# Seven products of half tiles in the last block of a gated-branch layer

## The reference

```python
h = rmsnorm(x, g_pre); proj = h @ w_in                 # 1024 x 10240
out_a = gmlp_spatial(a_u, layernorm(a_v)) * silu(a_z)
out_b = silu(layernorm(depthwise31(b_a * sigmoid(b_b)))) * silu(b_z)
out_c = multiscale_pool(c_x) * silu(c_z)
out_d = d_b * depthwise3(d_c * d_x) * silu(d_z)
merged = sum_i sigmoid(gate_i + b_i) * (out_i @ w_branch[i])   # 4 gates of width 1024
x + rmsnorm(merged @ w_out, g_post)                    # and the new states of the convolutions
```

## Time and profile before

| | |
|---|---|
| median of three runs | 2459.53 us |
| profiled execution, its own time | 2460.2 us |
| its span | 2458.1 us |
| PE busy (matmuls) | 2434.8 us, 99% |
| VectorE busy | 1258.1 us, 51% |
| ACT, POOL busy | 393.5 us, 329.2 us |
| mean rate of the DMAs | 215 GB/s |

### The profile page before, as it was taken

One profiled execution on the slowest core, in us unless ns is written; L12 is line 12 of the kernel. 1 busy time (PEld: TensorE's weight loads), 2 busy tenths in 40 slices (PEclk: granted clock), 3 DMA queues, 4 the chain that ended last, 5 costly groups with the idle time before them and its releaser, 6 DMA issues.

```text
span 2458.1 us, 34054 instructions
## 1 busy us (share of the span) xinstructions
PE 2434.8 (99%) x12772; PEld 2116.8 (86%) x12772; DVE 1258.1 (51%) x1923; ACT 393.5 (16%) x602; POOL 329.2 (13%) x173
## 2 busy tenths in 40 slices
PE   9999999999999999999999999999999999999998
PEld 7888887788888888888888888888899999999997
DVE  6776878752535455643344455654144545554323
ACT  5222222323011000111101000010201100000101
POOL 5435444444000000001000000000200000000000
PEclk9999999999999999999999999999999999999999
DMA  8868887787644555555654555555554344444457
GB/s 320 313 240 298 299 297 283 256 291 268 242 177 171 205 202 207 207 180 205 250 194 163 200 198 217 185 197 197 211 199 156 131 168 177 149 165 171 151 181 280
DMA packets 120382, 528.57 MB, mean 215 GB/s; under 512 B 11664, under 2 KB 14096, under 8 KB 74192
## 3 DMA queue, kind: packets, MB, share of 16 engines
q1 hardware_dynamic: 106032, 502.21, 57.1%
q10 hardware_dynamic: 14240, 24.89, 2.8%
HBM read 409.02 MB, written 118.03 MB: 214 GB/s over the span
## 4 chain that ended last, share of the span: by engine, by line
PE 96%; DVE 2%; issue 1%; DVEq 0%; POOL 0%; DMA 0%; ACT 0%; POOLq 0%; ACTq 0%
PE acc L1231 82%; PE acc L1474 6%; PE side L1369 4%; PE acc L1334 1%; PE side L1396 1%; PE side L1386 1%; PE side L1256 0%; DVE cb L791 0%; PE acc L1375 0%; PE side L1277 0%; DVE tmp L1026 0%; POOL w_pair L402 0%; DMA col<-in_cols 0%; DVE sq_y L1124 0%; DVE merged L1029 0%
## 5 line engine op out<-in xcount | busy, mean ns | idle before, releaser
L1231 PE MATMUL acc<-h_hi,w_pair 128*128 128x512 f32 (+1 forms) x5984 | 1553.3, 353 | 0.0
L1231 PEld LDWEIGHTS acc<-h_hi,w_pair 128*128 128x128 f32 x5984 | 1027.0, 188 | 142.3 <-issue 3.6
L1231 PE MATMUL acc<-h_lo,w_pair 128*128 128x512 f32 (+1 forms) x2992 | 951.4, 351 | 0.0
L1231 PEld LDWEIGHTS acc<-h_lo,w_pair 128*128 128x128 f32 x2992 | 529.3, 188 | 72.2 <-issue 3.6
L791 DVE SCALAR_TENSOR_TENSOR cb<-glu,col,cb 128x512 f32<-128x512 f32 x600 | 396.1, 725 | 23.2 <-issue 18.6
L1231 PE MATMUL acc<-out_hi,w_pair 128*128 128x512 f32 (+1 forms) x1280 | 346.5, 352 | 5.0 <-DVE tmp L1026 5.0
L402 POOL TENSOR_TENSOR w_pair<-w_raw,w_pair 128x512 fp32r<-128x512 f32 (+1 forms) x119 | 272.2, 2299 | 278.5 <-ACT w_pair L500 264.8
L1231 PEld LDWEIGHTS acc<-out_hi,w_pair 128*128 128x128 f32 x1280 | 221.3, 188 | 36.1 <-DVE tmp L1026 6.3
L1026 DVE TENSOR_TENSOR tmp<-acc,sig 128x512 f32<-128x512 f32 (+1 forms) x96 | 68.0, 708 | 342.2 <-PE acc L1231 340.3
L416 POOL TENSOR_TENSOR rstd<-msq,nhalf 128x5 f32<-128x5 f32 (+3 forms) x18 | 19.1, 1063 | 1648.0 <-DVE msq L725 797.7
L510 ACT ACTIVATE sig<-acc,col 128x512 f32<-128x512 f32 (+1 forms) x128 | 90.0, 703 | 896.3 <-PE acc L1231 894.3
(11 more groups left out here) (173 smaller groups left out, 1458.9 us busy)
## 6 DMA issues: line engine op xcount, KB each, us to landing
w_pair<-split_main SPq DMA_DIRECT2D x272, 1024.0 KB, 4.8
split_main<-w_pair SPq DMA_DIRECT2D x88, 1024.0 KB, 6.5
w_pair<-split_branch SPq DMA_DIRECT2D x96, 512.0 KB, 3.7
w_raw<-in_w_main SPq DMA_DIRECT2D x88, 512.0 KB, 5.1
split_branch<-w_pair SPq DMA_DIRECT2D x32, 512.0 KB, 6.5
w_raw<-in_w_branch SPq DMA_DIRECT2D x32, 256.0 KB, 5.6
xr<-in_x_t ACTq DMA_DIRECT2D x3, 2048.0 KB, 13.2
out_y_t<-xr ACTq DMA_DIRECT2D x6, 1024.0 KB, 7.7
```

The costliest lines, as they stand in the source:

```text
L1231: ins = pe.matmul(acc[:, s, b, 0:m], wt[slot][:, wk], mv_[:, k, t0:t0 + m], start=(k == 0 and n == 0), stop=(k == nk - 1 and n == 2))
```

## The change

In the last block the sections D, G1 and G3 are computed in pairs of row tiles. Two row tiles by two column halves, with the contraction in two halves, are a 2 x 2 product of blocks, A (weights) by B (frames). Seven products of blocks are made instead of eight:

S1 = A21 + A22, S2 = S1 - A11, S3 = A11 - A21, S4 = A12 - S2; T1 = B12 - B11, T2 = B22 - T1, T3 = B22 - B12, T4 = T2 - B21 (here with its sign turned, B21 - T2); the products A11 B11, S2 T2, S3 T3, S1 T1, A12 B21, S4 B22 and A22 T4, and VectorE's sums of them give the four result blocks.

- The S sums of all 16 pairs are made in blocks two and three, eight in each, in groups of four units from the second group of C to the first of G2: SP loads two raw row tiles (`s_load`), POOL adds, ACT rounds (`s_cast`), POOL subtracts, SP stores two pieces of 1 MB (`s_store`), once on every other group of four units.
- The T sums are made by VectorE and ACT in G0 of the last block, two steps behind each merged row tile.
- In the last block the ring's 4 MB are eight chunks of 0.5 MB; each product and each branch unit takes one chunk.
- The results of a pair are built in `zc` (four pieces of 288 columns) by VectorE and ACT; the gates' branch units go to `side`.
- Convolution steps move: eight instead of four ahead of V in the last block, four instead of eight in D. They stand ahead of each merge in G1.
- Loops that would hold a changing wait are written out; the load of two rows of LayerNorm weights moves to the last block.

```diff
@@ sync (SP): blocks two to four @@
+        def s_load(q):
+            if q == 0:
+                sp.wait_ge(w_lo_done, UPB)
+            else:
+                sp.wait_ge(s_stored, 32 * q)
+            for t in range(2):
+                sp.dma_start(w_raw[t][:, :], raw_rows(PAIR_TILE[q] + t)).then_inc(s_loaded, 16)
+        def s_store(q):
+            sp.wait_ge(s_lo_done, 2 * q + 2)
+            for n, part in enumerate((s_hi, s_lo)):
+                sp.dma_start(s_parts[q, :, n, :], f(part)).then_inc(s_stored, 16)
...
                 def body(i):
+                    q, phase = s_pair(j, UNIT0[name] // 4 + i)
                     for r in range(4):
                         u = u0 + i * 4 + r
+                        if phase == 0 and r == 0:
+                            s_load(q)
+                        if phase == 1 and r == 2:
+                            s_store(q)
...
@@ gpsimd (POOL) @@
+        def s_pair_sums(q):
+            pool.wait_ge(s_loaded, 32 * (q + 1))
...
+            pool.tensor_tensor(s1, a21, a22, ALU.add)
+            pool.tensor_tensor(s3, a11, a21, ALU.subtract)
+            pool.drain()
+            pool.tensor_tensor(s2, s1, a11, ALU.subtract)
+            pool.drain()
+            pool.tensor_tensor(s4, a12, s2, ALU.subtract)
+            pool.drain().then_inc(s_summed, 1)
+            for t in range(2):
+                pool.wait_ge(s_hi_done, 2 * q + t + 1)
+                pool.tensor_tensor(s_lo[:, t * DM:(t + 1) * DM], w_raw[2 + t][:, :], f(s_hi)[:, t * DM:(t + 1) * DM],
+                                   ALU.subtract).then_inc(s_lo_done, 1)
@@ scalar (ACT) @@
+        def s_cast(j, it, r):
+            q, phase = s_pair(j, it)
+            if phase == 0 and r == 2:
+                act.wait_ge(s_summed, q + 1)
+                for t in range(2):
+                    act.activation(s_hi[:, t * DM:(t + 1) * DM], w_raw[2 + t][:, :], ACT.Copy).then_inc(s_hi_done, 1)
...
@@ vector (DVE) @@
+            def pair_sums(name, p):
+                n = chunks_before(name, p)
+                bank = banks(name, p)
+                dve.wait_ge(p1_copied, p + 1)
+                dve.wait_ge(chunk_done, n + 2)
+                dve.tensor_tensor(c12, bank[1], c22, ALU.add).then_inc(pair_summed, 1)
+                dve.wait_ge(chunk_done, n + 3)
+                dve.drain()
+                dve.tensor_tensor(c21, bank[2], c12, ALU.add).then_inc(pair_summed, 1)
+                dve.wait_ge(chunk_done, n + 5)
+                dve.tensor_tensor(c11, bank[0], c22, ALU.add)
+                dve.drain()
+                dve.tensor_tensor(c12, bank[3], c12, ALU.add)
+                dve.tensor_tensor(c22, bank[3], c21, ALU.add).then_inc(pair_summed, 2)
+                dve.wait_ge(chunk_done, n + 6)
+                dve.drain()
+                dve.tensor_tensor(c12, bank[1], c12, ALU.add).then_inc(pair_summed, 1)
+                dve.wait_ge(chunk_done, n + 7)
+                dve.tensor_tensor(c21, bank[2], c21, ALU.add).then_inc(pair_summed, 1)
+            def section_done(n_sig):
+                dve.drain().then_inc(acc_done, 16)
+                for s in range(2):
+                    dve.drain().then_inc(acc_free[s], 8)
+                dve.drain().then_inc(sig_used, n_sig)
+            def seven_merge(name, conv_at=None):
...
+                for p in range(PAIR0[name], PAIR0[name] + 4):
+                    pair_sums(name, p)
+                    for t in range(2):
+                        m = 2 * (p - PAIR0[name]) + t
+                        if conv_at is not None:
+                            conv_step(j, m + conv_at)
+                        dve.wait_ge(chunk_done, chunks_before(name, p) + 8 + t)
+                        dve.wait_ge(pair_sig, sigs_before(name, p) + 1 + t)
+                        dve.drain()
+                        dve.tensor_tensor(tv(tmp, j), branch_bank(m), tv(sig[t], j), ALU.mult).then_inc(pair_used, 1)
...
+                section_done(8)
+            def seven_d(i):
...
+                pair_sums("D", p)
...
+                conv_step(j, 18 + i)
+                pair_sums("D", p + 1)
...
+                dve.drain().then_inc(pair_used, 2)
+                result(j, 0, i)
@@ tensor (PE) @@
+            def seven(name):
...
+                if name != "G1":
+                    for s in range(2):
+                        pe.wait_ge(acc_free[s], u0 // 2)
+                if name == "D":
+                    pe.wait_ge(t_lo_done, 4)
...
+                for p in range(PAIR0[name], PAIR0[name] + n_pairs):
...
+                    if name == "D":
+                        if p >= 2:
+                            pe.wait_ge(pair_used, 2 * (p - 1))
+                    elif name == "G1" and first:
+                        pe.wait_ge(pair_used, 2 * p)
+                    elif not first:
+                        pe.wait_ge(pair_summed, 6 * p - 2)
+                    product(n, h11, bank[0])
...
+                    product(n + 1, tt[2], bank[1])
...
+                    product(n + 2, tt[3], bank[2])
+                    product(n + 3, tt[1], bank[3])
+                    pe.wait_ge(p1_copied, p + 1)
+                    product(n + 4, h21, bank[0])
+                    pe.wait_ge(pair_summed, 6 * p + 1)
+                    product(n + 5, h22, bank[1])
+                    pe.wait_ge(pair_summed, 6 * p + 2)
+                    product(n + 6, tt[4], bank[2])
+                    if gated_:
+                        for t in range(2):
+                            m = 2 * (p - PAIR0[name]) + t
+                            if not first:
+                                pe.wait_ge(pair_used, 2 * p - 1 + t)
+                            branch_unit(n + 7 + t, OUTBUF[ph], m)
```

More of the change, by code:

```diff
@@ L49 @@
 NU = UPB * NBLK
+SEVEN = ["D", "G1", "G3"]
+PAIR0, CHUNK0, PAIR_TILE = {}, {}, []
+_c = 0
+for _n in SEVEN:
+    PAIR0[_n], CHUNK0[_n] = len(PAIR_TILE), _c
+    _k = dict(SECTIONS)[_n] // (4 if _n[0] == "G" else 2)
+    PAIR_TILE += [MAIN0[_n] + 2 * _p for _p in range(_k)]
+    _c += _k * (9 if _n[0] == "G" else 7)
+NPAIR = len(PAIR_TILE)
+NCHUNK = _c
+CHUNKS = 8
 A_U, A_V, A_Z, B_A, B_B, B_Z, C_X, C_Z, D_B, D_C, D_X, D_Z = range(12)
@@ L266, in build, with banks, branch_bank, chunks_before @@
     HALF = WMAX // 2
+    c11, c12 = zc[0][:, 0:HALF], zc[0][:, HALF:WMAX]
+    c21, c22 = zc[1][:, 0:HALF], zc[1][:, HALF:WMAX]
+    def banks(name, p):
+        if name == "D" and p % 2:
+            return [side[:, n // 2, n % 2 * 512:n % 2 * 512 + HALF] for n in range(4)]
+        return [acc[:, n // 2, n % 2, 0:HALF] for n in range(4)]
+    def branch_bank(m):
+        return side[:, m % 2, :].rearrange("p (a n) -> p a n", a=2)[:, :, 0:HALF]
+    def chunks_before(name, p):
+        return CHUNK0[name] + (p - PAIR0[name]) * (9 if name[0] == "G" else 7)
+    def sigs_before(name, p):
+        n_d = PAIR0["G1"]
+        return p // 2 if name == "D" else n_d // 2 + 2 * (p - n_d)
+    def s_pair(j, it):
+        n = (it - 4) // 2
+        if 0 < j < NBLK - 1 and it >= 4 and n < NPAIR // 2:
+            return (j - 1) * (NPAIR // 2) + n, (it - 4) % 2
+        return None, None
+    def unrolled(eng, j, start, end, body):
+        if j:
+            for i in range(start, end):
+                body(i)
+        else:
+            each(eng, start, end, body)
     HALF_TILES = [(0, P), (P, P), (2 * P, HALF - 2 * P)]
@@ L458, in _ @@
                 elif j:
+                    if name == "M" and not last:
+                        for q in range((j - 1) * (NPAIR // 2), j * (NPAIR // 2)):
+                            s_pair_sums(q)
                     if name == "G2" or name == "G3" and not last:
@@ L576, in _ @@
                     load_xres(j - 1)
+                if last and r == 1:
+                    act.wait_ge(s_stored, 32 * NPAIR)
+                    for dst, src in [(lnv_g_bc, rows[0:WB]), (lnv_b_bc, rows[WB:2 * WB])]:
+                        act.dma_start(dst, src.partition_broadcast(P)).then_inc(lnv_loaded, 16)
                 if j and r in (5, 7):
@@ L674, in _ @@
             gates("G2b", 46)
-            gates("G3", 48)
+            if last:
+                seven_gates("G3", q0 + 48)
+            else:
+                gates("G3", 48)
             u0 = ub + UNIT0["O"]
@@ L887, in _ @@
                 dve.tensor_copy(smp_g[:, :, :], glu[:, :, CH + BLK + DEC:2 * CH + BLK + DEC])
-            for t in range(4):
+            for t in range(8 if last else 4):
                 conv_step(j, t)
@@ L1003, in _ @@
                 if c % 2:
[L1004 removed]
+                    conv_step(j, (8 if last else 4) + c // 2)
             wn = width(min(j + 1, NBLK - 1))
@@ L1046, in body @@
                         dve.drain()
+                        if last and ph == 0:
+                            t_steps(m)
                 dve.drain()
@@ L1060, in split_merged @@
                 dve.tensor_tensor(lo, src, f(hi), ALU.subtract).then_inc(merge_ready, 1)
-            merge(0, 0, 4, conv_at=6)
```

(19 more changed lines are left out.)

259 lines of the change are left out of this document (229 added, 30 removed).

## The result

The changed kernel takes 2534.21 us (five runs, 2533.97 to 2536.94) against 2459.98 for the one before: ratio 1.0303, 95% interval 1.0292 to 1.0315, 3.0% slower. Forecast was 2524, range 2486 to 2546. The profiled execution has a span of 2532.2 us, 74.1 more than before.

A forecast was written before the change was run, and what follows sets the result against it. PE (the matrix engine) was taken as the bound, 99% busy. From 2459.5 us: minus 25.6 matmuls, plus 21.5 edges, 49.1 store waits and 19.2 clock gives 2523.7 us; range 2486 to 2546.

The forecast's parts named there:

- What bounds it: Whole kernel: PE is busy 99% of the span, so only matmuls removed and new PE waits change the time.
- What is removed: D, G1 and G3: 84 matmuls a pair instead of 96, 16 pairs, 25.6 us off (23 to 28).
- Edges of the last block: New PE waits at D, inside D, G1, G2, G3 and the output section: 21.5 us in sum (15 to 27).
- D's start: Last block: PE waits 6.2 us, as the last T subtraction stands behind the last merge and its convolution step.
- G3: Last block, G3's start: PE waits for both buffers, one merge product, 0.95 us.
- Blocks two and three: Weight load of r=2 lands late behind POOL's subtraction and SP's stores: 24.55 us a block, 49.1 in two (41 to 75).
- Chunks keep up: Last block: 0.524 MB per 1.60 us, 328 GB/s, is kept up; at 299 GB/s D would take 5.6 us more.
- The clock: After long PE waits the clock falls: 2.4 us lost behind each of eight waits above 4.0 us, 19.2 in sum.
- Eight waits: Six of 6.4 us in blocks two and three, D's 6.2 and G2's 5.2: 19.2 us of clock tails.
- the four of 3.0 to 3.65: Four shorter PE waits: no clock tail counted, 9.6 us kept for the range.
- tail at all twelve: Rival: the clock falls behind all twelve waits, the four shorter ones too; 2533.3 us, chance 0.14.

The follow-up runs named there:

- The first experiment: Changed kernel with SP's stores and raw load put behind the weight loads in blocks two and three; 2469.01 us, ratio 1.0034.
- the wait alone: Stores and raw load behind the loads, but SP's wait for the subtraction kept ahead of the load of r=2; 2492.26 us, ratio 1.0122.
- the edges moved: Changed kernel with earlier accumulator release, T subtractions ahead of the convolution step and later PE waits in the last block; 2509.00 us, ratio 1.0194.
- another kernel: Changed kernel without the S sums in blocks two and three, the last block reading other stored weights of that size; 2466.95 us, ratio 1.0025.

## Why the prediction was right, point by point

- **What bounds it.** As said, PE's waits and its pace make the change: the terms below, 0.5 in block one, 46.8 of waits and 17.7 beyond them in blocks two and three, and in the last block 23.5 of waits and 9.8 of slower matmuls less the 26.7 removed, come to 71.6 of the 74.1 us. The last 2.5 were not placed one by one; 1.1 of them are D's odd pairs (0.3 us each beyond their wait).
- **What is removed.** 84 matmuls take 11.13 us where 96 took 12.80: 1.67 a pair, 26.7 us for 16 pairs; forecast 25.6.
- **Edges of the last block.** D's start 6.2 (6.2 forecast), four waits of 0.6 in D, 2.5 in all (3.0), G1 3.3 (3.15), G2 5.0 (5.2), output 3.3 (3.3) and 0.5 for its weights. The T subtraction took 1.36 us (1.39). G3 is the one that was mis-sized: PE waited 3.1 us for chunks, not 0.95 for a release. The chunks of slots 4 to 7 wait for the last two units before; I had counted only the accumulator's release. In all 23.9, of which 0.4 was there before at the output section: 23.5 instead of 21.5.
- **Blocks two and three.** 46.8 us of waits in ten places, longest 6.4; forecast 49.1 in ten, longest 6.4. The load landed 16.7 us after the release where I had 17.25, by two errors that cancel: it was issued after 7.7 us, not 6.95, since SP needs 0.85 us to put out the two stores, and behind them it took 9.0 us, not 10.3. The first experiment shows that SP's order is the cause of all of it. My expectation for the wait alone took too little: 23 us, not under 6, since it delays r=0 of the next group too.
- **Chunks keep up** within the sections, as assumed: in D and G1 no wait on a chunk.
- **The clock.** The term that was mis-sized. Eight waits were to cost 2.4 us each, 19.2, and the four of 3.0 to 3.65 nothing. Behind the six of 6.05 to 6.39 us in blocks two and three PE lost 1.6, 2.3, 2.1, 2.8, 2.2 and 2.0 us (against the same stretches at full pace), behind D's 6.2 it lost 2.2 (84 matmuls in 13.56 us; 11.37 after the wait of 1.0 us with the edges moved) and behind G2's 5.0 it lost 3.0 (144 in 22.18 instead of 19.20): 18.2 us for the eight, nearly as forecast. The four that I counted at nothing cost 5.7: 2.4 at G1 (13.81 us), 1.7 at the output section (48 matmuls in 8.15 us instead of 6.4), 1.6 from G0 into D in block two (503 matmuls in 115.80 us) and nothing at the same place in block three, 114.21 us after a wait of 3.34 where block two's was 3.47. Another 3.1 us of the 17.7 that blocks two and three are longer beyond their waits stand in none of these stretches. With them the tails come to some 27 us against 19.2, most of the 10.5 us between forecast and result; the edges are 2.0 over, the waits 2.3 and the saved matmuls 1.1 the other way. The rival "tail at all twelve", 2533.3, comes within 1 us by its number, but that is luck: only three of those four had a tail. The granted clock of the two stretches behind the waits from G0 into D (852 to 857 us in block two, 1465 to 1470 in block three; the third column from the right):

```profile
852.00:857.00 5.00, 5.00 (x17) 3.97 (x16) 0.00 (x0) 0.00 (x0) 0.47 (x1) 0.68 1.02 426
1465.00:1470.00 5.00, 5.00 (x23) 4.14 (x22) 0.00 (x0) 0.00 (x0) 0.00 (x0) 1.00 1.02 421
```

  So a single number per wait was too simple. Over the six kernels here with this last block, the wait of 3.3 us at G1 cost nothing to 2.7 us, the 6.2 at D 1.6 to 2.6 and the 5.0 at G2 1.1 to 3.0. The Trainium skill (TensorE: Matmul & The Clock Gate, Loop structure matters more than you think) shows a DMA wait between bursts putting PE back to the low clock; this kernel's waits of 5.0 us and more agree, those near 3.3 us only in part, with the numbers above.

Left open: how the 42 us beyond the wait alone divide between the load's place behind the stores, the raw load's place and the clock behind the longer waits, which were not measured one by one; and why two waits of nearly the same length (3.47 and 3.34 us) leave the clock at different levels.

## What to carry to other kernels

A side job that is hidden on every engine still costs if its waits and its bulk stores stand ahead of the main stream's loads in the order of one issuer: put them behind the loads of the same step, the wait for the previous store too. When work is saved on the bound engine, look at what each section waits for at its start; here late releases and one late subtraction at the starts of D, G1, G2 and the output section ate 18 us of a 27 us saving and up to 10 more by the clock, and moving them ahead in VectorE's order gave 25 us back. Count the clock with each long stall of PE: those of 5.0 to 6.4 us cost 1.1 to 3.0 us beyond themselves here, those of 3.3 to 3.5 us between nothing and 3.0.

## What the hardware showed that I had not expected

- A stall of 3.3 us on PE at G1 can already lower the granted clock (13.81 us for 84 matmuls; 11.13 running on at full clock, 11.37 after a short stop) but need not (11.38 us in another kernel; 1.00 in block three), and matmuls with no use in the stall prevent it in seven of eight places: with 168 of them the kernel was 14.6 us faster, 11.9 of the trace's 15.5 us in the blocks where they stand.
- A DMA issuer that is held for 7 us and then sends 3.5 MB at once made a 1 MB load take 12.7 us; the median is 4.8.
